# A two-block fp32 model on one core: the first attention's transposes moved from TensorE to 32x32 pieces and transfers, and five smaller moves

## What is computed

```python
# first block
h = rms_norm(x, g_mix);  u, gb, gc, q, k, v = split(h @ w_in)      # six parts of 512 columns
y_conv = gb * short_conv(gc * u, conv_w)                           # causal, width 3
y_attn = dilated_mixture(rms_norm(q), rms_norm(k), v)              # 8 heads of 64, three dilations
x = x + concat(rms_norm(y_conv), rms_norm(y_attn)) @ w_out
x = x + (silu(h @ w_gate) * (h @ w_up)) @ w_down                   # h = rms_norm(x), 2816 hidden
# second block
h = rms_norm(x) * (1 + scale) + shift;  proj = h @ w_in_2          # state-space part and sparse attention
ya = (glu(gelu(s5_mixer(xa))) * silu(za)) @ w_a_o
yb = (dsa_mixer(q, k, v, ...) * silu(zb)) @ w_b_o                  # top 128 keys of each query, 8 heads
x = x + gate * ((sigmoid(ga) * ya + sigmoid(gb) * yb) @ w_out_2)
return rms_norm(x, final_g)
```

## Time and profile before

| | |
|---|---|
| median of 3 timed runs | 1007.5 us (1007.38 to 1007.88) |
| profiled execution, its own time | 1008.97 us |
| its span in the trace | 1007.4 us |
| TensorE busy | 987.2 us, 98% |
| VectorE, ScalarE, GpSimd busy | 680.3, 439.3, 155.2 us |
| mean granted TensorE clock | 0.994 |

### The profile page before, as it was taken

The page is one execution under the profiler, slowest core; times in us unless marked ns, Lnnn a source line. Parts: engine busy times, 40 slices in busy tenths (PEclk is TensorE's granted clock), DMA queues, the critical chain, the costliest instruction groups (busy, mean ns, idle before and its releaser), DMA issues.

```text
span 1007.4 us, 14453 instructions
## 1 busy us (share of the span) xinstructions
PE 987.2 (98%) x4734; PEld 802.0 (80%) x4734; DVE 680.3 (68%) x1210; ACT 439.3 (44%) x725; POOL 155.2 (15%) x270
## 2 busy tenths in 40 slices
PE   6999999999999999999999999999999999999996
PEld 6887787777888888888888886888888887767886
DVE  5786786797766656645526568498978764665655
ACT  4656667543333332332311236945552334553333
POOL 3000100110000000864000000835750000000000
PEclk8999999999999999999999999999999999999998
DMA  6245534252533233244232223332233332112322
GB/s 209 85 133 160 171 99 146 66 146 83 153 117 104 86 102 103 85 146 142 90 104 88 99 75 105 98 87 68 64 105 100 87 105 63 44 62 84 104 84 84
DMA packets 145168, 104.11 MB, mean 103 GB/s; under 512 B 4636, under 2 KB 136988, under 8 KB 145132
## 3 DMA queue, kind: packets, MB, share of 16 engines
q1 hardware_dynamic: 139792, 85.96, 28.6%
q0 software_dynamic: 5104, 17.64, 5.7%
q10 hardware_dynamic: 236, 0.06, 0.0%
HBM read 99.45 MB, written 4.19 MB: 103 GB/s over the span
## 4 chain that ended last, share of the span: by engine, by line
PE 95%; ACT 2%; DVE 1%; issue 1%; DMA 1%; SPq 0%; DVEq 0%; ACTq 0%
PE bank L573 19%; PE bank L575 19%; PE bank L574 19%; PE bank L819 4%; PE bank L818 4%; PE bank L817 4%; PE bank L550 3%; PE bank L557 2%; PE bank L558 2%; PE bank L559 2%; PE bank L639 2%; PE bank L726 1%; PE bank L728 1%; PE bank L727 1%; PE bank L613 1%
## 5 line engine op out<-in xcount | busy, mean ns | idle before, releaser
L573 PE MATMUL bank<-hH,wH 128*128 128x512 f32 x840 | 328.6, 391 | 0.0
L575 PE MATMUL bank<-hH,wL 128*128 128x512 f32 x840 | 326.9, 389 | 0.0
L574 PE MATMUL bank<-hL,wH 128*128 128x512 f32 x840 | 326.9, 389 | 0.0
L1051 ACT ACTIVATE wH<-raw 128x1024 fp32r<-128x1024 f32 x155 | 164.2, 1060 | 270.6 <-PE bank L575 134.9
L1491 DVE TENSOR_TENSOR wL<-raw,wH 128x1024 fp32r<-128x1024 f32 x155 | 196.5, 1268 | 125.5 <-ACT wH L1051 124.6
L573 PEld LDWEIGHTS bank<-hH,wH 128*128 128x128 f32 x840 | 157.7, 188 | 36.2 <-issue 2.4
L575 PEld LDWEIGHTS bank<-hH,wL 128*128 128x128 f32 x840 | 157.7, 188 | 33.0
L574 PEld LDWEIGHTS bank<-hL,wH 128*128 128x128 f32 x840 | 157.7, 188 | 32.2
L819 PE MATMUL bank<-aH,wL 128*128 (+1 forms) x176 | 68.5, 389 | 0.0
L817 PE MATMUL bank<-aH,wH 128*128 (+1 forms) x176 | 68.5, 389 | 0.0
L818 PE MATMUL bank<-aL,wH 128*128 (+1 forms) x176 | 68.5, 389 | 0.0
(11 more groups left out here) (465 smaller groups left out, 1520.0 us busy)
## 6 DMA issues: line engine op xcount, KB each, us to landing
raw<-in_w_in_dram SPq DMA_DIRECT2D x61, 512.0 KB, 3.5
mraw<-in_w_mod_dram POOLq DMA_DIRECT2D x24, 512.0 KB, 4.6
raw<-in_w_gate_dram SPq DMA_DIRECT2D x22, 512.0 KB, 3.6
raw<-in_w_up_dram SPq DMA_DIRECT2D x22, 512.0 KB, 3.5
raw<-in_w_down_dram SPq DMA_DIRECT2D x22, 512.0 KB, 3.2
raw<-in_w_out_dram SPq DMA_DIRECT2D x16, 512.0 KB, 3.5
x_tok<-in_x_dram SPq DMA_DIRECT2D x4, 512.0 KB, 7.4
rotations<-eb POOLq DMA_DIRECT2D x4, 512.0 KB, 5.1
```

The lines of the kernel that those rows point to most:

```text
L573: mm(o, a, hH[:, k, :], start=(k == 0), stop=False)
L574: mm(o, a, hL[:, k, :], start=False, stop=False)
L575: ins = mm(o, b, hH[:, k, :], start=False, stop=(k == KD - 1))
L1051: return A(o, i_, ACT.Copy, scale=scale)
```

## The change

1. **First attention.** The scores are plain fp32 matmuls on `qn` and `kn` for all four pairs, in the order block by block with the two heads side by side, with one negated-maximum at the end (`head_max`) where there was one for each head. In the three pairs of the loop the probabilities are turned by VectorE in 32 x 32 pieces into `turned`, and four transfers of GpSimd's queue carry the pieces to their partitions in `pTd`; TensorE multiplies from there. v's tokens are put in the order that this leaves, by ScalarE's copy of `vT`; for the last pair, which keeps TensorE's transposes, 16 small matmuls put them back. The folds 0 and 1 of `w_mod` move behind the turning.
2. **Second attention**: tanh ahead of the split of the next slot on ScalarE.
3. **Feed-forward entry**: VectorE's split of the up slot moves from before the last tile to between its two additions; TensorE does three blocks of the up slot ahead, not two.
4. **First load**: only the identity (64 KB) comes before x; the diagonal mask comes later on GpSimd's queue, and a third constant goes.
5. **Down projection**: the last two slots are interleaved, so that banks 0 to 3 close early; VectorE adds five squares, TensorE three.
6. **Tail**: features 768 to 1023 are projected with tokens on partitions: the activations are the stationary tile, the weights move in 256 columns, token block by token block. x's last two tiles are transposed ahead, the gate and the final gain come as rows by three small transfers.

```diff
@@ scores of the first attention
-                pe.wait_ge(q_lo, i + 1)
-                split_scores(i)
+                pe.wait_ge(qn_rdy, i * 2 + 2)
+                scores(i, qn, kn)
@@ TensorE
+            def attend_turned(a, v, vcol):
+                pe.wait_ge(turn_in, 16 * TB * (a + 1))
+                wait(pe, o_free, a + 1)
+                for kb in range(TB):
+                    for hh in range(2):
+                        r = slice(HD * hh, HD * hh + HD)
+                        ins = mm(OB[r, P * kb:S], v[:, kb, vcol(hh)],
+                                 pTd[:, :, place_of(hh, kb), :].rearrange("p i b c -> p b i c"),
+                                 start=(kb == 0), stop=(kb == TB - 1), skip_group_check=True)
...
+                pe.nop().then_inc(turn_used, 1)
@@ VectorE
+            def turn(hh, qb):
+                v.transpose(turned[:, :, places(hh, qb), :].rearrange("p j b c -> p b j c"),
+                            L[:, hh, CB[qb]:CB[qb + 1]].rearrange("p (b j c) -> p b j c", j=TB, c=32)
+                            ).then_inc(turn_rdy, 1)
-            def normalise(a):
+            def normalise(a, turning=None):
                 for hh in range(2):
...
+                    if turning is not None:
+                        if hh:
+                            turning()
+                        dve.wait_ge(pn, a * 2 + (hh + 1))
+                        dve.wait_ge(turn_used, a + 1)
+                        for b in range(TB):
+                            turn(hh, b)
@@ VectorE, mix
-                if not last:
-                    mod_rows(i, range(0, 2))
-                normalise(i)
+                normalise(i, None if last else lambda: split_lo(Slot(3, 3, 6, i).next()))
...
-                    split_lo(Slot(3, 3, 6, i).next())
+                    mod_rows(i, range(0, 2))
+                    split_lo(Slot(3, 4, 6, i).next())
                     mod_rows(i, range(2, 4))
-                    split_lo(Slot(3, 4, 6, i).next())
+                    split_lo(Slot(3, 5, 6, i).next())
                     mod_rows(i, range(4, 6))
-                    split_lo(Slot(3, 5, 6, i).next())
@@ GpSimd
+            def turned_moves(a):
+                pool.wait_ge(turn_rdy, 2 * TB * (a + 1))
+                pool.wait_ge(turn_used, a + 1)
+                settled(pool)
+                for q in range(TB):
+                    pool.dma_start(pTd[:, q].rearrange("p b c -> p (b c)"),
+                                   turned[32 * q:32 * q + 32].rearrange("p j b c -> p j (b c)")).then_inc(turn_in, 16)
-            def mod_loads(i):
+            def mod_loads(i, between=None):
                 for m in range(6):
+                    if m == 2 and between is not None:
+                        between()
@@ ScalarE, second attention
+                A(thg[:], PB[3][:], ACT.Tanh, bias=hbg[:, bass.ds(i, 1)], scale=0.5).then_inc(th_rdy, 1)
                 if not last:
                     act.wait_ge(glu_full, i * 16 + 32)
                 split_hi(s.next())
-                A(thg[:], PB[3][:], ACT.Tanh, bias=hbg[:, bass.ds(i, 1)], scale=0.5).then_inc(th_rdy, 1)
@@ feed-forward entry
                 mark(TT(xT[:, d, :], xT[:, d, :], wo1[:], AD))
+                if d == KD - 1:
+                    split_lo(sl.next())
...
-                if 0 < d < KD - 1:
+                if 0 < d < KD - 2:
                     split_lo(Slot(N_WO, d + 1).next())
-            project_two(N_FF, x1l, 1, 2, last_pairs)
+            project_two(N_FF, x1l, 1, 3, last_pairs)
@@ down projection
+                pe.wait_ge(lo_done, N_DN + KF - 1)
+                for d in range(KD // 2):
+                    block(0, d)
+                pe.wait_ge(lo_done, N_DN + KF)
+                for d in range(KD // 2):
+                    block(1, d).then_inc(dn_done, 1)
+                    ins = block(0, KD // 2 + d)
+                ins.then_inc(slot_used, 1)
+                for d in range(KD // 2, KD):
+                    block(1, d).then_inc(dn_done if d < KD - 1 else slot_used, 1)
@@ tail, VectorE (the functions for halves go)
+            def token_residual(t):
+                dve.wait_ge(tk_mm, t + 1)
...
+                mark(TT(tkp[:, t, :], OT[t][:, 0:QD], rows[:, 0:QD], MU))
+                need()
+                TT(tkx[:, t, :], tkp[:, t, :], out_tok[:, t, last], AD).then_inc(x3t, 1)
+                dve.wait_ge(x3t, t + 1)
+                mark(TT(out_tok[:, t, last], tkx[:, t, :], rows[:, QD:2 * QD], MU))
...
+            token_residual(0)
+            token_residual(1)
+            token_norm(0, slice(0, 2))
+            token_scale(0)
+            token_scale(1)
+            token_residual(2)
+            token_norm(1, slice(2, 3))
+            token_residual(3)
+            token_norm(2, slice(3, 4), lambda: token_scale(2))
+            token_scale(3)
```

More of the change, by code:

```diff
@@ L84 @@
 NV2 = 48
[L87 removed]
+C_ID, C_DG, C_M1, C_END = 0, 128, 256, 768
 def constants():
@@ L696, in mix @@
                 freed(pe, Slot(2, 0, 6, i))
-                transposes(PB[3], [vT[:, blkc(b)] for b in range(TB)]).then_inc(vtr, 1)
+                if last:
+                    for b in range(TB):
+                        for j in range(TB):
+                            ins = mm(PB[3][32 * j:32 * j + 32, blkc(b)], vT[:, P * b + j:P * b + P:TB], ident,
+                                     start=True, stop=True, skip_group_check=True)
+                    ins.then_inc(vtr, 1)
+                else:
+                    transposes(PB[3], [vT[:, blkc(b)] for b in range(TB)]).then_inc(vtr, 1)
                 pe.wait_ge(ss_rd, i * 2 + 2)
                 pe.wait_ge(xt_done, KD)
-                pe.wait_ge(q_lo, i + 1)
-                split_scores(i)
+                pe.wait_ge(qn_rdy, i * 2 + 2)
+                scores(i, qn, kn)
                 if not last:
@@ L799, in _, with down @@
                     project(Slot(N_FF, s, 2, i))
-            def down(i, first, last):
+            def down(i, first):
                 for s in range(2):
@@ L812, in down @@
                     for d in (range(KD) if not first or s else (2, 3, 4, 5, 6, 7, 0, 1)):
-                        a, z = first and s == 0, last and s == 1
+                        a = first and s == 0
                         if a and d == 0:
@@ L997, in _ @@
             project_two(N_O2, mg_done, 2, 2)
+            for s in range(2):
+                transposes((PB[4], PB[7])[s], [xT[:, KD - 2 + s, blkc(b)] for b in range(TB)]).then_inc(x2_tr, 1)
             with pe.Fori(0, KD // 2 - 2) as i:
@@ new lines, in token_products @@
+                if s:
+                    ins.then_inc(tk_mm, 1)
+            token_products(0, 0)
+            token_products(1, 0)
+            to_tokens(KD // 2 - 2)
+            token_products(0, 1)
+            token_products(1, 1)
+            pe.wait_ge(x2_ev, 2)
+            pe.wait_ge(gr_rdy, 1)
+            for t in range(TB):
+                ins = mm(FB[:, t:t + 1], gr[:, blkc(t)], ones[:, 0:1], start=True, stop=True)
+            ins.then_inc(fs_mm, 1)
+            for t in (2, 3):
+                pe.wait_ge(gfree[t % 2], Slot(N_O2, KD - 4 + t).gf)
+                for s in range(2):
+                    token_products(t, s)
@@ L1987, in _ @@
                 TT(xT[:, d, :], xT[:, d, :], PB[d][:], AD).then_inc(x1_rdy, 1)
-            dve.wait_ge(sq2_rdy, SQ_ADDED)
-            for b in sq2[1:SQ_ADDED]:
-                need(mark(TT(sq2[0][:], sq2[0][:], b[:], AD)))
+                if d in (2, 3):
+                    add_square(d - 1)
+            for k in range(3, SQ_ADDED):
+                add_square(k)
+            need()
             dve.nop().then_inc(sq2_sum, 1)
@@ new lines, in token_norm @@
+            def token_norm(j, c, between=None):
+                dve.wait_ge(tsq, c.stop)
+                dve.wait_ge(fs_mm, 1)
+                need()
+                TT(sm[:, c], sm[:, c], FB[:, c], AD).then_inc(tsum, 1)
+                dve.wait_ge(tsum, j + 1)
+                r, m, w = (slice(b + c.start, b + c.stop) for b in (4, 8, 12))
+                mean(sm[:, c], 1.0 / D, sm[:, m])
+                if between is not None:
+                    between()
+                dve.wait_ge(f_rs, j + 1)
+                need()
+                need(newton(sm[:, r], sm[:, m], sm[:, w]))
+                dve.nop().then_inc(r_fin, 1)
```

290 lines of the change are left out of this document (112 added, 178 removed).

## The result

The changed kernel takes 1023.5 us (1022.6 to 1024.9, 4 runs) against 1007.4 for the one before: a ratio of 1.0161, with an interval of 1.0143 to 1.0179. It is 16 us slower, where 1003.4 was forecast. Its profiled execution has a span of 1021.1 us.

What follows compares the result with a forecast made beforehand. TensorE, busy 987.2 of 1007.4 us, was taken as the bound. Terms 2.1 - 0.9 + 0.95 + 0.9 + 0.35 + 0.65 + 0 = 4.05 us off gave 1003.4 us, range 1001.6 to 1005.2, with A and B 999.8 to 1009.0.

Steps and rivals of the forecast that it cites:

- When the turned pieces arrive: First attention's loop: turning 1.65 us, four transfers 4.3 us, arrival at 78.6; TensorE, there at 76.9, waits 1.7 us.
- the slow bound: Transfer of the turned pieces: 211 GB/s at full share, 6.2 us, arrival 80.5; a loss of 3.6 us in the loop.
- The middle: Transfer of the turned pieces: 307 GB/s, the mean of GpSimd's queue, between bounds of 402 and 211 GB/s.
- Rival B: Turned pieces: each transfer reads only 32 partitions, which halves its rate; loop loses 3.6 us, 1009.1 us in all; chance 0.20.
- What queues behind the wait: Loop: block 2 of `w_mod` loads behind the pieces, a serial fold chain follows; gain 0.7 us a pair, 2.1 for three.
- T2 + 13.0: Loop: third slot can start 13.0 us after block 2 of `w_mod` is there (T2 = 80.3), at 93.3.
- T2 + 9.25: Loop's fold chain: folds 4 and 5 end 9.25 us after block 2 of `w_mod` is there; a load needs 5.0.
- the 2.1 us: Loop of the first attention: total gain forecast for its three pairs, 0.7 us a pair.
- Rival C: Loop: turning in pieces costs twice, VectorE is the bound; 1013.4 us, clock another 3 us a pair; chance 0.13 with clock.
- Last pair: First attention's last pair, which keeps TensorE's transposes: products start about 197.4 instead of 196.52, loss 0.9 us (0.3 to 2).
- Small moves: Edits outside first attention: tanh 0.95, feed-forward entry 0.9, first load 0.35, down projection 0.65, tail 0 us gained.

Runs made afterwards that it cites:

- the filler: Changed kernel with 24 unread matmuls of 512 columns on TensorE ahead of the wait for the turned pieces: 1023.6 us, ratio 1.0167.
- the small moves: Changed kernel with the first attention as in the kernel before, all else kept: 1003.5 us, ratio 0.9963; once more 1004.2 us, 0.9970.
- two repairs: Changed kernel with products with v behind the next pair's first projection: 1027.3 us; or with folds 0 and 1 and two loads ahead of the turning: 1032.9 us.
- both edits together: Changed kernel with products with v behind the next pair's first projection, and folds 0 and 1 with their loads ahead of the turning: 1015.8 us, ratio 1.0093.
- the early split: Kernel with both edits, u's evacuation and next split ahead, two queues (1003.7 us), then VectorE's third-slot split moved ahead of the second division: 1013.7 us, ratio 1.0065.

## Why the prediction was wrong

- **When the turned pieces arrive: the step that failed.** The turning is right (1.70 and 1.68 us for 1.65), and so is VectorE's end (69.4 us; the run is 2.55 us ahead at the scores, so 72.0 in my times, as forecast). The data's part is not: 8.8 us, where I took 4.3 (307 GB/s) and 6.2 as the slow bound. That alone moves the arrival from 78.6 to 83.1; measured, in my times, is 83.0. The middle was chosen "because its row is the same queue"; with the same queue and bytes and another choice of source partitions the wait fell from 18.3 to 3.7 us. Rival B named this rule, but took half the speed of the stores, and its price was that of my slow bound; 148 GB/s is less than its 211. The range was too narrow at this end, since that bound came from a window with other traffic, not from a row with such a source. My slow bound also left the load of block 2 behind the pieces at 1.7 us, the price at 307 GB/s; it came 2.8 us after them.
- **What queues behind the wait** was the right mechanism. With block 2 at 83.3, which is 85.8 in my times where I had 80.3, T2 + 13.0 gives a third slot at 98.8, a loss of 4.8 us a pair; measured are 6.2. The chain itself was too short: 14.1 us from fold 2 to the slot, not 13.0. Nearly all of that is in its first term, T2 + 9.25 for the end of fold 5, which took 10.2: block 5 landed 5.5 us after its issue, not 5.0, and issues follow the folds by some 0.6. The term also counts a split between folds 2 and 3 that the order of the program does not have. With 128 partitions read, pieces and block 2 come at 79.0 and 80.3 in my times, where I had 78.6 and 80.3; but the chain is 14.4 there, as block 5 lands 5.5 us after its issue, and the loop takes 127.6 us for 126.7. So even at my rate the 2.1 us would not have come: a gain of 0.7 a pair was less than the error of a chain of nine steps.
- **Rival C** had the direction and the point from which the chain of folds decides (block 2 after 81.7). Its cause, a turn of twice the cost, was wrong. Its number with the clock, 1013.4 and three times 3, is 1022.4, close to the measured 1023.5, and that is luck: the clock made products and sums 2.4 us a pair longer, but the filler shows that this cost nothing in the end, because the folds were just as late.
- **Last pair**: a loss of 0.8, forecast 0.9.
- **Small moves**, by the trace of them alone against before: tanh 1.0 (0.95); feed-forward entry 0.9 (0.9), and neither last tile is waited for; down projection 0.4 (0.65): one fp32 matmul less, 0.86, but from its first matmul to its sums it is 0.4 us longer; tail 1.1 (0): the last scaling comes 0.5 us early, not 1 us late as I had it, and what follows it is 0.7 us shorter, where I gave the one open store 1.2. First load 0.9 in time (0.35). Their sum is 4.3, measured 3.1 to 3.7. Part of the difference may be a slot of the second block's `w_a_o` that waits for its weights: 0 and 1.2 us in the two profiles of the small moves, up to 1.8 in others that have them, and nothing in the three profiles without them.
- The forecast for this part, 2.85 us, was near the 3.1 to 3.7, with errors of 1.1 and 0.55 us in the tail and the first load that the other terms hide only in part; the whole miss of 20 us is in the loop.

## What to carry to other kernels

Price a transfer by which partitions its source and its destination take, not by its queue or its bytes alone. Where no row of the trace has that shape, the range has to reach below the slowest row: here the measured rate was 0.7 of the slowest one, at full share. Count how many chains end within a microsecond of each other at the place that is being improved: here two did, and each of two repairs made things worse alone and better together. Before work is taken off TensorE in exchange for a transfer, ask what TensorE can do until the transfer's slow case; here one projection was not enough in one queue (2.2 us of wait a pair) and was enough in two.

## What was not expected of the hardware

In the first pair, with the weights beside it, the four transfers from 32 neighbouring partitions ran at 148 GB/s, those from 32 partitions four apart at 258, those from 128 partitions at 270; in the other two pairs at 136 to 139, 306, and 304 to 311. Two queues moved the same pieces in 8.1 us instead of 9.3, on average over the pairs.

TensorE's clock was granted at half after some 4 us of idleness in a wait of 5.65 us, and stayed full in waits of 1.7 and 1.9 us. In between the length of the wait did not decide: with both edits together, waits of 2.20 and 2.19 us left it full and one of 2.12 us was followed by half. The fall then comes when TensorE is at work again: after a wait of 2.53 us that ended at 84.10 (the early split) the clock was still 1.00 from 82 to 84, was 0.82 from 84 to 86 and 0.50 from 86 to 88, and the products took 3.4 us instead of 2.4.
